# Splits three ahead, gate multiply on VectorE, final norm's sums two units on, x in four DMAs

## The reference

```
def layer(l, x, mem_k, mem_v, st):
    h = rmsnorm(x, norm_mix_g[l])
    u = h @ w_in[l]                      # split into the inputs of four mixers
    y_a, y_b, y_c, y_d = rglru(...), ssd(...), gated_delta(...), s5(...)   # recurrences over chunks of 64 tokens
    x = x + concat(y_a, y_b, y_c, y_d) @ w_out[l]
    x = x + cross_attend(rmsnorm(x, norm_cross_g[l]), mem_k, mem_v, w_cq[l], w_co[l])   # 4 heads, 256 memory tokens
    x = x + swiglu(rmsnorm(x, norm_ffn_g[l]), w_ffn_gate[l], w_ffn_up[l], w_ffn_down[l])
    return x, states

def swiglu(h, w_gate, w_up, w_down):
    return (silu(h @ w_gate) * (h @ w_up)) @ w_down      # hidden width 2816

y_prompt = rmsnorm(xp, norm_final_g)
y_sample = rmsnorm(xs, norm_final_g)
```

## Time and profile before

| | before |
|---|---|
| runs | 4242.36, 4240.63, 4239.75 us; median 4240.63 |
| profiled execution | 4238.34 us, span 4236.5 us, mean granted TensorE clock 0.927 |
| TensorE (PE) busy | 3748.2 us, 88%, 24,250 matmuls |
| VectorE (DVE) | 2228.1 us, 53% |
| ScalarE (ACT) | 1255.2 us, 30% |
| GpSimd (POOL) | 320.8 us, 8% |
| DMA | 942.08 MB, mean 222 GB/s |

### The profile page before, as it was taken

How to read it: one execution, slowest core, us unless ns; L and a number is a source line. 1 busy time by engine, 2 the same in 40 slices (tenths; PEclk the granted TensorE clock), 3 DMA queues, 4 the chain that set the end, 5 groups by cost and what they waited for, 6 DMA issues and landing times.

```text
span 4236.5 us, 63633 instructions
## 1 busy us (share of the span) xinstructions
PE 3748.2 (88%) x24250; PEld 3627.6 (86%) x24250; DVE 2228.1 (53%) x4752; ACT 1255.2 (30%) x2291; POOL 320.8 (8%) x340
## 2 busy tenths in 40 slices
PE   5587868898788899997899997899998899998998
PEld 5586867798788899997899997899998799998998
DVE  7576644167773545563555554554455455543323
ACT  4344332145432322222323232323232322322101
POOL 0010000001100001100101100001010001100000
PEclk8798977689999999998999998999999999999999
DMA  7755585479968456567555666556666655566776
GB/s 246 239 170 175 175 299 209 130 266 364 350 247 275 163 195 220 206 219 251 191 195 210 220 221 220 208 197 210 212 223 221 216 177 206 199 212 246 244 251 216
DMA packets 372574, 942.08 MB, mean 222 GB/s; under 512 B 35120, under 2 KB 168752, under 8 KB 371760
## 3 DMA queue, kind: packets, MB, share of 16 engines
q1 hardware_dynamic: 372272, 938.03, 63.6%
HBM read 763.32 MB, written 174.57 MB: 221 GB/s over the span
## 4 chain that ended last, share of the span: by engine, by line
PE 54%; DVE 16%; DMA 11%; PEld 6%; DVEq 4%; ACT 3%; issue 3%; SPq 2%; ACTq 0%; PEldq 0%
PE banks L441 15%; PE banks L442 14%; PE banks L443 14%; DMA uc_dram<-uc_sb 3%; DVE m_p_sb L2073 2%; DMA kept_dram<-wlo_sb 2%; DMA wlo_sb<-kept_dram 2%; PEld banks L443 2%; DVE uc_sb L1131 2%; PEld banks L441 2%; PEld banks L442 2%; PE banks L1512 1%; PE banks L1518 1%; DVE wlo_sb L1040 1%; PE banks L1521 1%
## 5 line engine op out<-in xcount | busy, mean ns | idle before, releaser
L441 PE MATMUL banks<-hh_sb,whi_sb 128*128 128x384 f32 (+2 forms) x3552 | 1216.0, 342 | 162.2 <-DVE wlo_sb L1040 58.1
L442 PE MATMUL banks<-hh_sb,wlo_sb 128*128 128x384 f32 (+2 forms) x3552 | 1181.8, 333 | 0.0
L443 PE MATMUL banks<-hl_sb,whi_sb 128*128 128x384 f32 (+2 forms) x3552 | 1180.2, 332 | 0.0
L441 PEld LDWEIGHTS banks<-hh_sb,whi_sb 128*128 128x128 f32 x3552 | 696.6, 196 | 193.1 <-issue 69.1
L442 PEld LDWEIGHTS banks<-hh_sb,wlo_sb 128*128 128x128 f32 x3552 | 697.1, 196 | 2.1 <-issue 1.2
L443 PEld LDWEIGHTS banks<-hl_sb,whi_sb 128*128 128x128 f32 x3552 | 696.0, 196 | 0.0
L441 PE MATMUL banks<-g_hi_sb,whi_sb 128*128 128x384 f32 (+2 forms) x1568 | 541.9, 346 | 77.6 <-DVE g_lo_sb L1151 30.1
L442 PE MATMUL banks<-g_hi_sb,wlo_sb 128*128 128x384 f32 (+2 forms) x1568 | 528.4, 337 | 0.0
L443 PE MATMUL banks<-g_lo_sb,whi_sb 128*128 128x384 f32 (+2 forms) x1568 | 528.3, 337 | 0.0
L441 PEld LDWEIGHTS banks<-g_hi_sb,whi_sb 128*128 128x128 f32 x1568 | 316.5, 202 | 91.2 <-DVE g_lo_sb L1151 33.3
L1232 DVE TENSOR_TENSOR x_sb<-x_sb,banks 128x384 f32<-128x384 f32 (+2 forms) x400 | 202.4, 514 | 330.9 <-PE banks L443 327.4
(11 more groups left out here) (411 smaller groups left out, 5143.7 us busy)
## 6 DMA issues: line engine op xcount, KB each, us to landing
whi_sb<-kept_dram SPq DMA_DIRECT2D x560, 512.0 KB, 3.7
wlo_sb<-kept_dram SPq DMA_DIRECT2D x560, 512.0 KB, 4.8
raw_sb<-w SPq DMA_DIRECT2D x144, 512.0 KB, 5.0
kept_dram<-whi_sb SPq DMA_DIRECT2D x112, 512.0 KB, 6.5
kept_dram<-wlo_sb SPq DMA_DIRECT2D x112, 512.0 KB, 7.3
uc_dram<-uc_sb SPq DMA_DIRECT2D x90, 192.0 KB, 3.4
ldb_sb<-x_t SPq DMA_DIRECT2D x72, 192.0 KB, 4.6
x_sb<-x_t SPq DMA_DIRECT2D x5, 1536.0 KB, 9.2
```

The lines of the kernel that those rows point to most:

```text
L441: eng.matmul(out, xh, yh, start=first, stop=False)
L442: eng.matmul(out, xl, yh, start=False, stop=False)
L443: return eng.matmul(out, xh, yl, start=False, stop=last)
```

## The change

Five edits:

- `SPLIT_AHEAD` goes from 2 to 3 and `LOAD_AHEAD` from 4 to 5. The slots stay four, the raw buffers three.
- The final norm's `st` follows unit 11, `final` the units 12 to 15 (the final norms of passes 0 to 3).
- GpSimd's multiply of the gate moves to VectorE, behind the SiLU, in `dve_second`; `gs_done` goes.
- The low half of the turned probabilities (`pt`) is taken from the bank in the section itself, no more in `dve_second` of the next.
- x is loaded by four DMAs of two row blocks, in units 16 and 17 and in the two `z` sections, each when its pair of y blocks is stored (`out_stored` is now four semaphores). In passes 0 and 5 the four stand together in `w`.

```
-SPLIT_AHEAD, LOAD_AHEAD, KEPT_AHEAD = 2, 4, 2
+SPLIT_AHEAD, LOAD_AHEAD, KEPT_AHEAD = 3, 5, 2
...
-            at = a.index(units[9]) + 1
+            at = a.index(units[11]) + 1
             a[at:at] = [st]
-            for e, u in zip(end, units[10:]):
+            for e, u in zip(end, units[12:]):
...
+            elif unit is not None and unit.kind == "g":
+                g = gs[:, unit.a % 2, 0:n]
+                eng.wait_ge(g_gated, unit.ev + 1)
+                eng.tensor_tensor(g, g, rstd[:, unit.ni % 2, 0:n], ALU.mult)
+                eng.drain()
...
-            elif s.kind == "pt":
-                wide = prompt_at(s.p)[1] * P
-                for mt in range(2):
-                    ...
-                    eng.drain().then_inc(free[(s.f + mt) % 3], 1)
...
             elif s.kind == "w":
                 if s.a == 0:
-                    eng.wait_ge(x_loaded, 16 * (s.p + 1))
+                    eng.wait_ge(x_loaded, 64 * (s.p + 1))
...
+            elif s.kind == "pt":
+                wide = prompt_at(s.p)[1] * P
+                for mt in range(2):
+                    slot = s.a % 2 * 2 + mt
+                    eng.wait_ge(g_hi_done, s.g + mt + 1)
+                    eng.tensor_tensor(g_lo[:, slot, 0:wide], banks[:, (s.f + mt) % 3, 0:wide],
+                                      g_hi[:, slot, 0:wide].bitcast(F32), ALU.subtract).then_inc(g_lo_done, 1)
+                    eng.drain().then_inc(free[(s.f + mt) % 3], 1)
...
             elif s.kind == "up":
-                eng.wait_ge(gs_done, HID * s.p + s.a + 1)
                 bank = bank_in(eng, s.f)
...
         def pool_section(eng, i):
-            unit = evicted_at(i)
-            if unit is not None and unit.kind == "g":
-                g = gs[:, unit.a % 2, 0:cols(unit.p)]
-                eng.wait_ge(g_gated, unit.ev + 1)
-                eng.tensor_tensor(g, g, rstd[:, unit.ni % 2, 0:cols(unit.p)], ALU.mult).then_inc(gs_done, 1)
+            pass
...
-        def sp_x(eng, p):
+        def sp_x(eng, p, q):
             if p:
-                eng.wait_ge(out_stored, 16 * KD * p)
-            else:
+                eng.wait_ge(out_stored[q], 32 * p)
+            elif q == 0:
                 eng.wait_ge(sample_stored, 16 * 5)
-            t0, n = PASSES[p][0] * P, cols(p)
-            eng.dma_start(x[:, :, 0:n], t["x_t"][:, :, t0:t0 + n]).then_inc(x_loaded, 16)
+            t0, n, at = PASSES[p][0] * P, cols(p), slice(2 * q, 2 * q + 2)
+            eng.dma_start(x[:, at, 0:n], t["x_t"][:, at, t0:t0 + n]).then_inc(x_loaded, 16)
...
-            if s.kind == "u" and s.b == 16 and s.p >= 2:
-                sp_x(eng, s.p - 1)
+            if s.p >= 2 and (s.kind == "u" and s.b >= 16 or s.kind == "z"):
+                sp_x(eng, s.p - 1, s.b - 16 if s.kind == "u" else 2 + s.a)
             elif s.kind == "w" and s.a == 0:
-                if s.p in (0, NP - 1):
-                    sp_x(eng, s.p)
+                for q in range(KD // 2 if s.p in (0, NP - 1) else 0):
+                    sp_x(eng, s.p, q)
```

More of the change, by code:

```diff
@@ L615, in program @@
         s_max, s_exp, p_done = sem("s_max"), sem("s_exp"), sem("p_done")
-        gs_done, up_done = sem("gs_done"), sem("up_done")
-        out_ready, out_stored = sem("out_ready"), sem("out_stored")
+        up_done = sem("up_done")
+        out_ready, out_stored = sem("out_ready"), [sem(f"out_stored{q}") for q in range(KD // 2)]
         qs_done, ps_done, pst_done = sem("qs_done"), sem("ps_done"), sem("pst_done")
@@ L1418, in sp_section @@
                     eng.wait_ge(out_ready, KD * s.p + k + 1)
-                    eng.dma_start(t["y_t"][:, k, t0:t0 + n], x[:, k, 0:n]).then_inc(out_stored, 16)
+                    eng.dma_start(t["y_t"][:, k, t0:t0 + n], x[:, k, 0:n]).then_inc(out_stored[k // 2], 16)
         per_chunk = dict(
@@ L2692, in _ @@
             sp.wait_ge(finals_stored, 16 * len(outs))
-            sp.wait_ge(out_stored, 16 * KD * NP)
+            for stored_pair in out_stored:
+                sp.wait_ge(stored_pair, 32 * NP)
             sp.wait_ge(sample_stored, 16 * 5)
```

## The result

The changed kernel takes 4319.4 us (median of 4 runs, 4315.59 to 4327.61) against 4240.19 before (4 runs): ratio 1.0184, interval 1.017 to 1.0199, so 79 us slower. The forecast was 4279, slower, with a range from 4216 to 4330. The direction and the main cause held; the forecast change was 38 us, so the size was off by a factor of two.

The account below looks back on a forecast made before the run. TensorE, busy 88%, was taken as the bound, its first-use stretches paced by a four-slot split-and-store loop. Terms 43 + 9 + 6 + 1 + 7 − 23 − 5 = +38 us gave 4279 us, range 4216 to 4330.

Parts of the forecast that it names:

- The loop: Feed-forward of pass 0: store behind a later raw load, turn spans two weights, not three; 5.0 us a weight, +43 us.
- Its signs: Feed-forward of pass 0: ScalarE's store waits grow to about 90 us, stretch 340 to 375, low-half stores land in 6 to 7.
- w to vo: 545 to 678 us of pass 0: 24 weights at 5.0 us fit, but waits delay the exponentials; +9 us (0 to +26).
- the length of a turn: Split loop: slower pace shortens landing and queueing, so a turn falls from 11.67 to 10.0 us.
- two windows: Trace stretches behind the landing estimate: low half's store lands in 7.9 us at 397 GB/s, 5.9 at 303.
- z and the start: z of pass 0: second weight waits for its section's first store, +6 us; start: a third split stands ahead, +1.
- The sums: Final norm two units later: four of TensorE's six waits for the sums shrink; −23 us (0 to −26.5).
- Rival C: Final norm: the wait for sums becomes a wait for banks, so −23 becomes 0, 4302 us; chance 0.12.
- x: x in four DMAs: less queueing for kept weights against three added issues on SyncE; −5 us (−16 to +5).
- Gate: Gate multiply on VectorE: 23 TensorE waits get 0.53 us longer each; +7 us (−3 to +25).
- Rival A: Split loop doesn't bind: landing 5.9 us or less, holds hide, feed-forward about −2; 4216 to 4219 us; chance 0.20.
- Rival B: Split loop: queue stays full at 7.9 us, 5.8 a weight, holds add up; +104 us, 4345; chance 0.13.

Follow-up runs that it names:

- the lead alone: Kernel before with splits three instead of two and raw loads five instead of four ahead, nothing else: 4330.75 us, ratio 1.0212.
- loads four ahead: Changed kernel with splits still three ahead but raw loads four instead of five ahead: 4222.07 us, ratio 0.9954.
- the store in front: Changed kernel, splits three and loads five ahead, with each section's stores put in front of its raw load on SyncE: 4226.14 us, ratio 0.997.
- the run with one store: Kernel before with splits three and loads five ahead, storing only each pair's high half (later passes left wrong): 4282.87 us, ratio 1.0093.
- the gate alone: Kernel before with only the gate multiply moved to VectorE, run twice: 4243.59 us, ratio 0.9998, and 4246.61 us, ratio 1.0005.
- the changed kernel with `2, 4, 2`: Changed kernel with splits two and raw loads four ahead again: 4227.71 us, ratio 0.9963.
- the sums and x: Kernel before with only the final norm's sums two units later and x loaded in four DMAs: 4228.74 us, ratio 0.9965.

## Why the prediction was right and wrong

**The loop.** Right in mechanism and place: the store behind a raw load one weight further on, a turn over two weights instead of three. The runs with the lead alone, with loads four ahead and with the store in front show it from three sides. Its signs came out a little beyond their upper ends: ScalarE's waits 124.6 us for about 90, the stretch 376.5 for 340 to 375, the landing 7.1 for 6 to 7.

The measured change of the two spans is 45 us more than the sum. Of these 19 lie in the feed-forward of pass 0, 18 in w to vo and 8 in the memory part; x and the gate, with about 10 us in opposite directions, cancel.

**What failed first: the length of a turn.** The step was "a landing of some 6.5 … with 0.3 less of queueing gives a turn … = 10.0, or 5.0 a weight". In the trace of the changed kernel the turns of the feed-forward (from low half n+2 to low half n+4) have a mean of 11.3 us, with the lead alone 11.1, so a weight takes 5.5 to 5.6. The low half's store lands in 7.1 us (median of 67; mean 6.9) at 289 GB/s, not in 5.9 to 6.5, against 7.6 in the same stretch before:

```profile
kept_dram<-wlo_sb SPq DMA_DIRECT2D x67, 512.0 KB, 7.1
```

I had read the landing as a function of the mean rate, from two windows. It goes rather by the DMAs still in flight, that is, issued before the store and not yet landed. With at most two (its own raw load and high half) a low half's store took 6.0 us on average before (8 stores) and 5.8 in the changed kernel (10); with five or more 7.9 (45) and 7.6 (17). The first window has stores of the short kind: at 888.92 one left 0.9 us behind its raw load, with nothing else in flight, and landed in 5.75. The burst that a store leaves in is the same in both kernels, and its place there is worth 1.3 us (the run with one store). What the slower pace takes away is only a part of the older transfers, since the pairs come at uneven intervals (from under 4 to over 8 us): 4.9 were in flight on average, now 3.7, and the landing is shorter by 0.5.

So 0.4 us of the 1.3 us that are missing in the turn are landing. Another 0.7 are ScalarE and VectorE, which are not free at once when the store lands: ScalarE starts 0.3 us after it on average, and from there to the end of the low half it takes 2.8 us instead of the 2.3 of the earlier trace rows. The one turn that I started from was also a short one: before, the 20 turns that a store closed have a mean of 12.3, not 11.67.

By the prediction's own sum 68 × 5.5 = 374, or +59, is the end at which all other holds hide in the loop, and +61.9 came. That 374 is near the 376.5 measured proves nothing by itself, since 5.5 is a stretch divided by its weights; what shows that the loop sets most of the stretch are the 51 of 68 splits that waited for a store. I had made the turn too short (68 × 0.5 = 34 us) and counted 18 us of holds on top, two errors that partly cancel.

**What failed next: w to vo.** "24 × 5.0 = 120 fits into 133" gave +9; +27.4 came, just over my bound of 26, and 23.3 of it in `s`, `pt` and `vo`. The sum took every loop for one over two weights. Each section `s` uses two weights. Both raw loads stand in front of both stores, the second waits for split n+3, and the store of weight n behind it frees the slot for split n+4, the very next one, so the loop spans one weight there. From the timelines of SyncE, ScalarE and VectorE:

```profile
635.40 1.22 DVE L1040 TENSOR_TENSOR wlo_sb<-raw_sb,whi_sb 128x1024 fp32r<-128x1024 f32 x1 [0.69 <-ACT whi_sb L856]
...
636.65 0.32 SPq L1303 DMA_DIRECT2D raw_sb<-vo_dram  x1
...
637.49 0.43 SPq L1284 DMA_DIRECT2D kept_dram<-wlo_sb  x1
...
643.76 1.06 ACT L856 ACTIVATE whi_sb<-raw_sb 128x1024 fp32r<-128x1024 f32 x1 [8.39 <-DMA kept_dram<-wlo_sb]
```

The store of 637.49 landed in 6.2 us and ScalarE split at once; the low half is done at 646.08. That is a turn of 9.5 us over one weight. Then the exponentials run, then comes the next split. A section with two weights takes 13.7 us (636.62 to 650.30 at the low halves), where before the same turn, 9.1 us, spanned both of its weights (608.23 to 617.34). The split that waits stands ahead of the exponentials on ScalarE, and TensorE waits for these.

**z and the start.** +4.6 for +6, −0.1 for +1. The 7.8 us in the memory part I had at 0, without a reason. The lead alone has +4.8 there and the kernels with both leads as before −2.9 to −5.5, so it is the lead's; no run says through what.

**The sums.** −20.3 for −23, and the waits fell to 6.9 us, as said. Rival C, that nothing comes of it, is what happens when the edit stands alone, by another way than C's: not banks, but the load of x. The forecast had "behind stores of `final` that are later by two units" only as a remark to x, with no price; alone it was worth 16.6 us, and with x in quarters z has only +2.6.

**x.** −5 for +4.8, and 0 alone. The +4.8 isn't x's: `w` of passes 1 to 5 has +5.0 of it, and +4.9 with the lead alone, where x is one DMA. What x is worth stands in the paragraph above.

**Gate.** +7 for −4.6 in the later passes, but these −4.6 are not the gate's either: the gate alone has −0.7 there, and the lead alone, without it, −6.4. In all, nothing that can be told from zero. The rule of the Trainium skill on the ports (SBUF — State Buffer, "Who interferes with whom") would have made it −2; no run here tells the two apart.

**Turned probabilities.** No run of its own; `s`, `pt` and `vo` of passes 1 to 5 differ by at most 0.7 us a pass, and the changed kernel with `2, 4, 2` is as fast as the sums and x without this edit and the gate.

**Rival A** needed a landing that falls with the rate, to 5.9 or less; it stayed at 7.1. **Rival B** had the turn almost right (5.8) and, with "sends its transfers in bursts", a good part of the reason, but its holds on top were not there: 407 us for the 376.5 measured.

## What to carry to other kernels

When a lead is lengthened, look at what the longer-leading instruction waits for and at what stands behind it in its queue: a buffer's release that is queued behind a wait for later work closes a loop, and its pace is the turn divided by the number of weights that it spans. Count the span in both versions, and separately for sections that use two weights, before pricing anything else. Take the landing time from transfers with as many others in flight, not from a window with a lower mean rate. An edit that shows nothing alone may be two effects that cancel: compare stage by stage before dropping it, and take the scatter of a stage from runs that don't touch it.

## What the runs showed of the hardware

A 512 KB store to DRAM that stands third behind two other 512 KB transfers, mostly within 1.5 us, lands in 7.1 us at a mean of 289 GB/s and in 7.6 at 348 (medians of 67): a sixth less traffic gave 0.5 us. What it found in flight was worth more: 5.8 to 6.0 us on average with at most two DMAs, 7.6 to 7.9 with five or more.

TensorE's granted clock over the feed-forward of pass 0 was 0.94 with 15% idle time (47.5 of 315 us) and 0.87 with 23% (87.3 of 376.5), and the same matmuls were busy for 22 us more. The share of idle time alone doesn't give the clock: it was 0.83 with 34% idle in 18 to 137 us and 0.66 with 27% in 545 to 678.
